# High-part products first on tiles that are still being split, and other places for token sums and last tiles, in a kernel of three transformer blocks

## What is computed

```python
# block 1, its end: output product, residual, final norm
x = x + merged @ w_out;  x = rmsnorm(x, final_g)
# block 2
n = rms_norm(x, mix_norm_g)
proj = n @ w_in                      # q, k, v, bg, cg, xh, su, sv
mixed = concat(attention, gated_conv, spatial_gating(su, sv))
x = x + group_rms_norm(mixed) @ w_out
x = x + square(relu(rms_norm(x, mlp_norm_g) @ w_up)) @ w_down
x = rms_norm(x, final_norm_g)
# block 3
u = x @ w_in                         # mLSTM q, k, v, gates, output gate, pooling input
x = layer_norm(ALPHA * x + concat(y_mlstm, y_pool) @ w_out)
x = layer_norm(ALPHA * x + square(relu(x @ w_ff1)) @ w_ff2)
```

## Time and profile before

| | |
|---|---|
| Median of 3 runs | 3708.53 us (3706.79 to 3709.82) |
| The profiled execution | 3709.7 us, of which the span of the trace 3708.4 us |
| PE busy | 3641.9 us, 98% of the span |
| DVE, ACT, POOL busy | 1762.1, 1152.9, 1098.4 us |
| Chain that ended last | PE 90%, DVE 7%, issue 2%, ACT 1% |
| Mean granted TensorE clock | 0.994 of 2.4 GHz |

### The profile page before, as it was taken

One profiled execution on the slowest core, in us unless ns is written; L12 is line 12 of the kernel. 1 busy time (PEld: TensorE's weight loads), 2 busy tenths in 40 slices (PEclk: granted clock), 3 DMA queues, 4 the chain that ended last, 5 costly groups with the idle time before them and its releaser, 6 DMA issues.

```text
span 3708.4 us, 42437 instructions
## 1 busy us (share of the span) xinstructions
PE 3641.9 (98%) x17740; PEld 3006.2 (81%) x17740; DVE 1762.1 (48%) x2289; ACT 1152.9 (31%) x1491; POOL 1098.4 (30%) x747
## 2 busy tenths in 40 slices
PE   7999999999999999999999999999999999999998
PEld 6999987888888877887888888877777778888886
DVE  6676616999643473344522222227556642222226
ACT  5555522222231344443411111125232331111113
POOL 4333411222233441113522222225113432222223
PEclk9999999999999999999999999999999999999998
DMA  2100121111242341012311111113112211111112
GB/s 105 35 29 29 33 88 40 57 57 52 85 153 91 102 134 36 25 36 80 97 46 50 47 46 51 46 57 122 35 40 74 69 63 46 51 46 46 49 49 74
DMA packets 65134, 229.31 MB, mean 62 GB/s; under 512 B 7216, under 2 KB 7472, under 8 KB 64944
## 3 DMA queue, kind: packets, MB, share of 16 engines
q1 hardware_dynamic: 64944, 226.60, 18.7%
HBM read 201.40 MB, written 25.17 MB: 61 GB/s over the span
## 4 chain that ended last, share of the span: by engine, by line
PE 90%; DVE 7%; issue 2%; ACT 1%; POOL 0%; DMA 0%; SPq 0%; DVEq 0%; ACTq 0%
PE psum L524 79%; PE psum L647 2%; PE psum L917 1%; PE psum L884 1%; PE psum L899 1%; PE psum L618 1%; DVE fb L2160 0%; PE psum L771 0%; PE psum L733 0%; PE psum L671 0%; PE psum L670 0%; DVE hl L2091 0%; DVE pb L2950 0%; DMA X<-in_xin 0%; DVE Ab L2195 0%
## 5 line engine op out<-in xcount | busy, mean ns | idle before, releaser
L3208 POOL TENSOR_TENSOR wl<-raw,wh 128x512 fp32r<-128x512 f32 x636 | 888.5, 1417 | 2301.8 <-ACT wh L1229 2301.7
L524 PE MATMUL psum<-hh,wh 128*128 128x512 f32 (+2 forms) x3760 | 1202.9, 391 | 19.7 <-POOL wl L3208 9.1
L524 PE MATMUL psum<-hh,wl 128*128 128x512 f32 (+2 forms) x3760 | 1163.3, 380 | 0.0
L524 PE MATMUL psum<-hl,wh 128*128 128x512 f32 (+2 forms) x3760 | 1159.0, 379 | 0.0
L524 PEld LDWEIGHTS psum<-hh,wh 128*128 128x128 f32 x3760 | 679.6, 189 | 168.9 <-issue 36.2
L524 PEld LDWEIGHTS psum<-hl,wh 128*128 128x128 f32 x3760 | 695.7, 189 | 131.7
L524 PEld LDWEIGHTS psum<-hh,wl 128*128 128x128 f32 x3760 | 697.1, 189 | 127.0
L1229 ACT ACTIVATE wh<-raw 128x1024 fp32r<-128x1024 f32 x318 | 335.1, 1054 | 775.3 <-PE psum L524 772.4
L524 PE MATMUL psum<-hdh,wh 128*128 128x512 f32 x1024 | 334.8, 399 | 5.0 <-DVE B L3109 4.4
L524 PE MATMUL psum<-hdl,wh 128*128 128x512 f32 x1024 | 332.0, 396 | 0.0
L524 PE MATMUL psum<-hdh,wl 128*128 128x512 f32 x1024 | 331.8, 396 | 0.0
(11 more groups left out here) (436 smaller groups left out, 2958.7 us busy)
## 6 DMA issues: line engine op xcount, KB each, us to landing
raw<-in_wts SPq DMA_DIRECT2D x318, 512.0 KB, 3.5
keep_x<-B SPq DMA_DIRECT2D x14, 512.0 KB, 6.0
X<-in_xin SPq DMA_DIRECT2D x8, 520.0 KB, 5.6
keep_sz<-tmp SPq DMA_DIRECT2D x8, 512.0 KB, 2.9
tmp<-keep_sz SPq DMA_DIRECT2D x8, 512.0 KB, 4.1
av<-keep_gr SPq DMA_DIRECT2D x8, 512.0 KB, 3.2
av<-keep_gc SPq DMA_DIRECT2D x8, 512.0 KB, 3.7
xc<-keep_x SPq DMA_DIRECT2D x8, 512.0 KB, 5.6
```

The source lines that it names most:

```text
L524: ins = pe.matmul(out, w, x[:, k, c0:c0 + width], start=first and n == 0, stop=final and n == 2)
L3208: gp.tensor_tensor(wl[:, s, a], raw[:, s, a], fp(wh[:, s, a]), SUB).then_inc(*c.lo.tick(i, p))
```

## The change

No operation is added or left out; the number of matmuls and all waits for data that are needed stay. It moves four kinds of things.

1. **High parts first.** `three` gets an argument `only`, which picks some of its three products. A new `fresh_half` replaces `gemm_half` for the first half slab of each half at `SGU`, `MLP2`, `GATES3` and `MLP3`: the product `wh*hh` of tile k waits for `wh` and for `hh` of that tile alone, `wh*hl` follows two tiles behind, and all eight `wl*hh` stand at the end. The two slabs of `OUT3` are written out: the first takes `wh*hh` and `wl*hh` of a tile as its high part comes, `wh*hl` two tiles behind, the second slab runs four tiles behind (three before), and the last tile's products of both come at the end.
2. **`gemm_late`** for slab `OUT3 + 2`: its products with `wl` run three tiles behind the others.
3. **Later sums.** The jobs for half 1 pass more turns before the token sums: `rest_out` 6 to 11, `rest_square` 4 to 11, `rest("v1", 1)` 5 to 13. The last pooling product (`last_pool`) waits 11 turns where it was 4. The spreads keep their distance behind the sums.
4. **Tile 7 earlier on ACT.** At the four places ACT writes the high part of tile 7, half 0, before the square of output tile 7 of half 1 and (but for `GATES3`) before the split of the next slab.

```diff
-        def three(pr, hd, i, k, kw, first, final, xh, xl, off, halves=(0, 1), lead_free=None):
+        def three(pr, hd, i, k, kw, first, final, xh, xl, off, halves=(0, 1), lead_free=None, only=(0, 1, 2)):
...
-            if (i, kw // 4) not in split_in:
+            if 1 not in only and i not in split_in:
+                split_in.add(i)
+                pe.wait_ge(*c.hi(i))
+            if 1 in only and (i, kw // 4) not in split_in:
                 split_in.add((i, kw // 4))
                 pe.wait_ge(*c.lo(i, kw // 4))
...
+        def gemm_late(i, until):
+            pr = grab(pairs, (i, 0), until)
+            for n in range(KT + 3):
+                if n < KT:
+                    three(pr, None, i, n, n, n == 0, False, hh, hl, META, only=(0, 2))
+                if n >= 3:
+                    ins = three(pr, None, i, n - 3, n - 3, False, n == KT + 2, hh, hl, META, only=(1,))
+                    if n < KT + 2:
+                        side.turn()
...
+        def fresh_half(i, hf, until, ver):
+            pr = grab(pairs, (i, 0), until)
+            for n in range(KT + 2):
+                if n < KT:
+                    pe.wait_ge(*c.h_hi(ver, n, hf))
+                    three(pr, None, i, n, n, n == 0, False, hh, hl, META, (hf,), only=(0,))
+                if n >= 2:
+                    pe.wait_ge(*low_done(ver, n - 2, hf))
+                    three(pr, None, i, n - 2, n - 2, False, False, hh, hl, META, (hf,), only=(2,))
+                    if n % 2:
+                        side.turn()
+            for k in range(KT):
+                ins = three(pr, None, i, k, k, False, k == KT - 1, hh, hl, META, (hf,), only=(1,))
+                if k % 2 and k < KT - 1:
+                    side.turn()
+            ins.then_inc(*c.gemm.tick(i, 0))
+            side.turn()
...
         def rest_out(hf):
-            yield from pause(6)
+            yield from pause(11 if hf else 6)
...
         def rest_square(st, hf):
-            yield from pause(4)
+            yield from pause(11 if hf else 4)
...
         def last_pool():
-            yield from pause(4)
+            yield from pause(11)
...
         def rest(st, hf):
-            yield from pause(5)
+            yield from pause(13 if (st, hf) == ("v1", 1) else 5)
...
-        for m in (2, 3):
-            gemm(OUT3 + m, c.ev_v("x3", m))
+        gemm_late(OUT3 + 2, c.ev_v("x3", 2))
+        gemm(OUT3 + 3, c.ev_v("x3", 3))
...
+        last_high(7, 0)
         half_square("v1", 7, 1, c.ev_v("x3", 7, 1))
         split(MLP3 + 1)
-        last_high(7, 0)
```

More of the change, by code:

```diff
@@ L522, in three @@
                 for n, (w, x) in enumerate(((a, xh), (b, xh), (a, xl))):
+                    if n not in only:
+                        continue
                     for out, c0, width in g:
-                        ins = pe.matmul(out, w, x[:, k, c0:c0 + width], start=first and n == 0, stop=final and n == 2)
+                        ins = pe.matmul(out, w, x[:, k, c0:c0 + width], start=first and n == only[0], stop=final and n == only[-1])
             return ins
@@ L540, in gemm, with gemm_half @@
             side.turn()
-        def gemm_half(i, hf, until, ver=None):
+        def gemm_late(i, until):
[24 more added lines that the diff above has]
+                    side.turn()
+            ins.then_inc(*c.gemm.tick(i, 0))
+            side.turn()
+        def gemm_half(i, hf, until):
             pr = grab(pairs, (i, 0), until)
             for k in range(KT):
-                if ver:
-                    pe.wait_ge(*low_done(ver, k, hf))
                 ins = three(pr, None, i, k, k, k == 0, k == KT - 1, hh, hl, META, (hf,))
@@ L931, in tensor @@
                 until = c.ev("sv", n, hf) if n < 2 else c.ev("su", n - 2, hf)
-                gemm_half(SGU + 4 * hf + n, hf, until, "nx2" if n == 0 else None)
+                if n == 0:
+                    fresh_half(SGU + 4 * hf, hf, until, "nx2")
+                else:
+                    gemm_half(SGU + 4 * hf + n, hf, until)
             if hf == 0:
@@ L996, in first_ups @@
                 for u in range(4):
-                    gemm_half(base + 4 * hf + u, hf, c.ev("up", base, u, hf), ver if u == 0 else None)
+                    if u == 0:
+                        fresh_half(base + 4 * hf, hf, c.ev("up", base, 0, hf), ver)
+                    else:
+                        gemm_half(base + 4 * hf + u, hf, c.ev("up", base, u, hf))
                 side.drain()
@@ L1045, in tensor @@
                 until = (c.ev("gates", hf), c.ev("pre", 0, 0, hf), c.ev("pre", 0, 1, hf), c.ev("v3", 0, hf))[n]
-                gemm_half(GATES3 + 4 * hf + n, hf, until, "nx3" if n == 0 else None)
+                if n == 0:
+                    fresh_half(GATES3 + 4 * hf, hf, until, "nx3")
+                else:
+                    gemm_half(GATES3 + 4 * hf + n, hf, until)
             side.drain()
@@ L1156, in tensor @@
         side.add(last_pool())
-        duo(OUT3, "cat", [c.ev_v("x3", 0), c.ev_v("x3", 1)], order=CAT_ORDER)
+        prs = [grab(pairs, (OUT3 + e, 0), c.ev_v("x3", e)) for e in range(2)]
+        for n in range(KT - 1 + 4):
+            if n < KT - 1:
+                k = CAT_ORDER[n]
+                pe.wait_ge(*c.h_hi("cat", k))
+                three(prs[0], None, OUT3, k, k, n == 0, False, hh, hl, META, only=(0, 1))
+                side.turn()
+            if 2 <= n < KT + 1:
+                k = CAT_ORDER[n - 2]
+                pe.wait_ge(*low_done("cat", k))
+                three(prs[0], None, OUT3, k, k, False, False, hh, hl, META, only=(2,))
+            if n >= 4:
+                k = CAT_ORDER[n - 4]
+                three(prs[1], None, OUT3 + 1, k, k, n == 4, False, hh, hl, META)
+                side.turn()
+        k = CAT_ORDER[-1]
+        pe.wait_ge(*c.h_hi("cat", k))
+        three(prs[0], None, OUT3, k, k, False, False, hh, hl, META, only=(0, 1))
+        pe.wait_ge(*low_done("cat", k))
+        three(prs[0], None, OUT3, k, k, False, True, hh, hl, META, only=(2,)).then_inc(*c.gemm.tick(OUT3, 0))
+        three(prs[1], None, OUT3 + 1, k, k, False, True, hh, hl, META).then_inc(*c.gemm.tick(OUT3 + 1, 0))
         side.drain()
@@ L1848, in scalar @@
                 square("n6", 2 * j, c.ev_v("dn", MLP2, 7, 2 * j, hf), hf)
+            if hf:
+                in_high(7, 0)
             square("n6", 7, c.ev_v("dn", MLP2, 7, 7, hf), hf)
         split(GATES3 + 1)
-        in_high(7, 0)
         half_mean_root("n6", 1)
```

4 lines of the change are left out of this document (2 added, 2 removed).

## The result

| | median | runs | profiled execution, its span |
|---|---|---|---|
| before | 3708.78 us | 3702.96 to 3710.66 (19) | 3708.4 us |
| after | 3714.28 us | 3712.30 to 3717.18 (19) | 3714.6 us |

The ratio is 1.0018, 95% interval 1.0012 to 1.0024: 5.5 us slower, within the 0.2% (7.4 us) that the prediction took for no change, though the interval leaves out a ratio of 1. The forecast was 3709.0, the range 3701 to 3716. One of the 90 runs of the kernel before that were taken along with the experiments lasted 5190.6 us at a mean clock of 0.703; it is left out of what follows.

The account below looks back on a forecast made before the run. The prediction took TensorE, 98% busy, as the bound, with time to win only in its waits. From 3708.4: -7.2 OUT3, -0.5 GATES3, +2.7 SGU, +3.5 MLP3, +2.0 clock gave 3708.9, or 3709.0 for runs; range 3701 to 3716.

Parts of the forecast that it names:

- OUT3: At OUT3, waits for low parts and the half clock behind them go, about 0.5 us stays: 7.2 us less.
- GATES3: At GATES3, the first slab ends 1.0 us sooner, a later split gives back 0.5: 0.5 us less.
- SGU: At SGU, later sums make PE wait 2.5 us for wl before the third half slab; overall 2.7 us more.
- the sign: At SGU and MLP3, DVE would start the second half's norm 4 to 5 us later.
- rival 4: Slower: ACT waits for late sums, splits come late, the clock falls after each; 3716.5 us, chance 0.13.
- MLP3: At MLP3, 3.7 us won in the first half slab is given back through late sums, spread and norm: 3.5 more.
- (1): MLP3's first half slab: POOL's last low part takes 1.3 us, nine matmuls follow; it ends 3.7 us sooner.
- (2): MLP3's third slab: PE waits 2.2 us for wl; the late spread makes DVE's norm of half 1 4.3 late.
- Clock: New half clock at MLP3's first slab, none at SGU: 2.0 us added in all, bounds 0 and 5.
- the first sentence of the prediction: Whole kernel: PE is 98% busy, so time can only go or come where TensorE waits.
- The rival in which the clock stays at 2.4 GHz: The clock does not fall in the short waits, so the 2.0 us is not added: 3707 us, chance 0.20.
- Rivals 1 and 2: First: nothing given back, 3688 us, chance 0.08. Second: DVE catches up at MLP3, 3702 us, chance 0.11.

Follow-up runs that it names:

- x2_out3_only: The kernel before with only the written-out OUT3 slabs, last_pool at 11 turns and gemm_late: 3700.16 us, 7.9 below before.
- x3_no_out3: The kernel after with the OUT3 parts undone (duo, last_pool at 4, plain gemm for OUT3 + 2): 3721.78 us, 13.7 above before.
- x4_v1_back: The kernel after with only the place of the sums at MLP3 undone (rest v1, 1 from 13 back to 5): 3705.47 us, 2.6 below before.
- y3_mlp3_fresh: x2_out3_only plus, at MLP3 alone, high parts first in both first half slabs and tile 7 first on ACT: 3703.98 us, 3.9 below before.
- y4_mlp3_joined: y3_mlp3_fresh plus one wait: MLP3's first half slab begins only when tile 6's high part is there; 3698.88 us, 9.0 below before.
- x1_pauses_back: The kernel after with the three later places of the token sums undone (11, 11, 13 back to 6, 4, 5): 3706.58 us, 1.5 below before.
- w2_all_fresh_joined: x1_pauses_back plus the one wait for tile 6's high part before MLP3's first half slab: 3699.55 us, 8.1 below before.

## Where the prediction was right, and where not

- **The number**: the forecast of no change holds in part by luck. It was the sum of places that were missed by 3 and 4 us in the same direction, while the band of 7.4 us is wide enough for that; a gain of 7.7 us and losses of 15 nearly cancel. That the kernel came out slower, by an interval that leaves out 1, was not forecast.
- **OUT3**: forecast 7.2 less; 7.7 between the traces, 7.9 (x2_out3_only) and 8.2 (x3_no_out3) by runs. No wait for a low part over 0.8 us and no half clock is left there, as named; the 0.5 us that was to stay did not.
- **GATES3**: 0.5 less against 0.3 measured; **MLP2** nothing, as said.
- **SGU**: forecast 2.7 more, measured 5.6. The two waits came as described (1.6 and 2.9 us in starts, forecast 1.1 by the same sum and 2.5). The step that failed is the sentence that put this wait beside the 2.69 us at `GATES3`, after which the clock stayed. It fell, for 6.6 us with PE busy 5.9 of them: half of that, 3.0 us, is about the whole gap. The spread came 7.6 us later than before where the forecast had 5.2, DVE's norm behind it 8.3 (the sign said 4 to 5). A stretch at 0.50 at `SGU` is what the prediction itself named as showing it wrong, for rival 4. Why the clock held in the earlier trace rows at 2525 and not here can be said only as the rows have it: here PE had six matmuls in the 3.3 us before, there three in 3.4. That points the other way, so the busy time of one such stretch does not decide it, and the cause stays open.
- **MLP3**: forecast 3.5 more and 2.0 for the clock, measured 9.5. The steps that the prediction names came, at other sizes, and one came that it does not have (3). Times of the forecast are given less the 2.2 us won ahead of `MLP3`. (1) The first half slab kept 1.5 us of the forecast 3.7 and ended at 2951.7, not 2949.7: its last low part took 1.72 us on POOL, not the 1.3 of the sum, and the stretch at 0.50 with PE busy 3.16 us cost 1.6. (2) The third slab's wait is 2.4 as against 2.2, but it came 2.0 late from (1), and the six matmuls ahead of the spread took 0.43 us each instead of 0.23, another 1.2. So the spread stands at 2964.11, where the forecast gives 2960.7, and DVE starts the norm of half 1 8.2 us later than before, not 4.3. (3) The fourth half slab's wait of 2.2 us was not foreseen. Its chain is on ACT (timelines of DVE and of ACT in the kernel after):

```profile
2965.59 0.69 DVE L3083 TENSOR_TENSOR B<-B,psum 128x512 f32<-128x512 f32 x1 [6.84 <-PE psum L656]
...
2967.33 0.72 ACT L2067 ACTIVATE hh<-B,vec 128x512 fp32r<-128x512 f32 x1 [7.37 <-DVE B L3086]
2968.71 0.72 ACT L2067 ACTIVATE hh<-B,vec 128x512 fp32r<-128x512 f32 x1 [0.66 <-DVE B L3086]
2969.34 0.58 ACT L1832 ACTIVATE t<-psum 128x512 f32<-128x512 f32 x1
2969.82 1.05 ACT L1297 ACTIVATE wh<-raw 128x1024 fp32r<-128x1024 f32 x1
```

  The eviction of the second half slab and the split for the fourth (the last two rows) stand behind two high parts of half 1, and these wait for the norm that waits for the spread. The prediction followed the late spread to DVE and to the last low part, but not to what is queued behind the first high parts on ACT. x4_v1_back shows that the waits of (2), (3) and (4) go with the place of the sums. (4) The late spread makes the last low part of half 1 late: 3.0 us in the first slab there, and a third stretch at 0.50.
- **Clock**: forecast 2.0 us in all, at one place. At these places the half clock lasts 16.5 us where it had been 10.0, and y3_mlp3_fresh against y4_mlp3_joined (5.1 us), x1_pauses_back against w2_all_fresh_joined (6.6 us), show that scattering the waits of `MLP3`'s first half slab alone costs 5 to 7, give or take 2. Of this, the starts in the two pairs of traces move apart by 4.5 and 3.9 us at `MLP3` itself. The rival in which the clock stays at 2.4 GHz (3) falls. So does the first sentence of the prediction, that time can only go or come where TensorE waits: it also went where the same waits were followed by a slower clock.
- **Rivals 1 and 2** fall: the waits for `wl` are there. **Rival 4** had the mechanism of `SGU`; the measured 3714.3 lies between it (3716.5) and the forecast. Rival 5, that the order makes no difference, falls with x2_out3_only and y3_mlp3_fresh against y4_mlp3_joined.
- The parts by runs, each against before: `OUT3` -7.9; high parts first with tile 7, +6.4 (x1 less x2); the late sums, +7.0 (after less x1). Their sum is the measured 5.5 by construction, since each run is the start of the next step. By the table of clocks the late sums are 10.4 us more of the rest and 2.7 less of half clock. High parts first with tile 7 is the largest miss: the prediction's own steps had the first half slabs some 5 us sooner (0.6, 1.0 and 3.7), with one half-clock stretch on the other side. It did not ask what scattered waits cost against a joined one.

## What to carry to other kernels

Where an engine must wait for a chain on other engines, joining its waits into one ahead of the work can be worth more than starting each piece as its data comes: here no less time was waited, and the clock fell early, or not at all, rather than in the work that ends last. One profiled execution does not price such a place; the mean clock of all runs does it better. A side job that starts a chain over several engines (sums, root, spread, norm) may stand as late as its result is first needed and no later; before moving it, follow everything queued behind each engine's wait for it, evictions and splits too. And a wait at an engine in order is often only the first of several: see what is late next before taking it away.

## What the runs showed of the hardware

- The granted clock fell to 1.2 GHz behind waits of 0.8 and 1.3 us and within one of 1.45 that followed each other (kernel after, 2943 to 2948). Behind one wait of 3.28 us it stayed at 2.4 GHz in y4_mlp3_joined and fell in w2_all_fresh_joined. With the same order of instructions and the same waits at `SGU` (1.4 and 0.6 us) it fell in x1_pauses_back and did not in w2_all_fresh_joined, so one profiled execution does not tell what a place costs in the median.
- The clock also fell where TensorE did not wait: in every trace it is at 0.50 for 3.4 us at three or four places between 2590 and 2800 us, with PE busy all the while (in the kernel before near 2608, 2670 and 2731). What brings it down there was not looked into; every kernel has it.
- At 1.2 GHz a matmul of 512 columns started every 0.43 us instead of 0.23, and eight sums of one column took 1.70 us instead of 0.95: short matmuls lose as much as long ones.
- POOL's low part of tile 7 took 1.72 us at 2946.26 in the kernel after, with DVE busy on operations with two inputs beside it, where it took 1.29 in the earlier trace rows; DVE's `acc<-acc,t` beside it took 1.75 us, and 0.68 at 2940.71 with POOL idle. That the two slow each other was not tried by a run.
